# Later layer norms of a two-block transformer kernel: centred rows turned by a product with a diagonal, and the residual made inside the next stage

## The reference

```
first block, layer i in 0..1:
  h = x*(1+sc_m)+sh_m;  y = mixer(h)          # convolutions, 1024-wide products
  x = layer_norm(ALPHA*x + (1+g_m)*y, mix_ln_g[i], mix_ln_b[i])
  h = x*(1+sc_f)+sh_f;  y = mixture_of_32_experts(h)
  x = layer_norm(ALPHA*x + (1+g_f)*y, ffn_ln_g[i], ffn_ln_b[i])
second block, layer l in 0..1:
  x = layer_norm(ALPHA*x + 0.5*swiglu(x, ffn1_in, ffn1_out), ln_g[l,0], ln_b[l,0])
  x = layer_norm(ALPHA*x + hybrid_mixer(x, ...),             ln_g[l,1], ln_b[l,1])
  x = layer_norm(ALPHA*x + 0.5*swiglu(x, ffn2_in, ffn2_out), ln_g[l,2], ln_b[l,2])
layer_norm(v, g, b) = (v - mean(v)) * rsqrt(var(v) + 1e-5) * g + b
```

## Time and profile before

| what | value |
|---|---|
| median of 3 runs | 2887.1 us |
| the profiled execution: its time / its span | 2888.29 us / 2886.5 us |
| TensorE matmul busy | 2541.2 us, 88% |
| VectorE / ScalarE / GpSimd busy | 43% / 29% / 15% |
| mean granted TensorE clock | 0.965 |
| first block / second block in the span | about 0 to 1424 / 1424 to 2886 us |

### The profile page before, as it was taken

One profiled execution on the slowest core, in us unless ns is written; L12 is line 12 of the kernel. 1 busy time (PEld: TensorE's weight loads), 2 busy tenths in 40 slices (PEclk: granted clock), 3 DMA queues, 4 the chain that ended last, 5 costly groups with the idle time before them and its releaser, 6 DMA issues.

```text
span 2886.5 us, 38313 instructions
## 1 busy us (share of the span) xinstructions
PE 2541.2 (88%) x15512; PEld 1772.3 (61%) x15513; DVE 1245.1 (43%) x2035; ACT 844.1 (29%) x1391; POOL 438.0 (15%) x462
## 2 busy tenths in 40 slices
PE   6989888988697888888699899988989989998997
PEld 3653322322584322332299788878979978887897
DVE  5562212110655111210254675556455467555645
ACT  2231100010231100001144344444444434444443
POOL 2210000000210010000020222333012032233301
PEclk9999999999897999999999999999999989999899
DMA  9979999999643999999855453344545535334552
GB/s 350 335 304 393 393 394 394 394 393 394 204 173 130 394 394 394 393 394 393 317 176 187 131 161 118 117 146 162 189 146 184 195 122 166 109 117 142 166 185 73
DMA packets 388354, 716.18 MB, mean 248 GB/s; under 512 B 18881, under 2 KB 192625, under 8 KB 382033
## 3 DMA queue, kind: packets, MB, share of 16 engines
q1 hardware_dynamic: 384048, 707.77, 68.6%
q10 hardware_dynamic: 2336, 3.52, 0.4%
q0 software_dynamic: 1792, 2.42, 0.3%
HBM read 709.69 MB, written 1.05 MB: 246 GB/s over the span
## 4 chain that ended last, share of the span: by engine, by line
PE 51%; DMA 27%; DVE 7%; issue 7%; POOL 5%; ACT 1%; SPq 1%; ACTq 0%; DVEq 0%; POOLq 0%
DMA ring<-in_e_w_down_dram 25%; PE w L702 17%; PE y L714 10%; PE w L706 8%; PE w L913 5%; PE w L899 2%; DMA ring<-in_ada_w_dram 2%; PE w L1150 1%; PE y L940 1%; DVE vv L1373 1%; DVE small L1364 1%; SPq L636 1%; POOL arena L2399 1%; PE w L1135 1%; PE w L882 1%
## 5 line engine op out<-in xcount | busy, mean ns | idle before, releaser
L1262 DVE TENSOR_TENSOR wsp<-ring,wsp 128x1024 fp32r<-128x1024 f32 x464 | 607.0, 1313 | 400.9 <-ACT wsp L1251 400.6
L702 PE MATMUL w<-hh,wsp 128*128 128x256 f32 x5056 | 685.2, 289 | 27.0 <-DVE wsp L1262 18.7
L702 PEld LDWEIGHTS w<-hh,wsp 128*128 128x128 f32 x5056 | 650.5, 196 | 52.5 <-issue 22.6
L1251 ACT CAST wsp<-ring 128x1024 fp32r<-128x1024 f32 x470 | 489.3, 1045 | 401.1 <-PE w L706 249.7
L899 PE MATMUL w<-ring,arena 128*64 128x512 f32 x2048 | 474.2, 600 | 64.9 <-DMA ring<-in_e_w_up_dram 57.4
L706 PE MATMUL w<-hl,wsp 128*128 128x256 f32 x2528 | 358.5, 284 | 5.4 <-DVE hl L1318 5.4
L899 PEld LDWEIGHTS w<-ring,arena 128*64 128x64 f32 x2048 | 135.8, 136 | 368.0 <-issue 213.5
L706 PEld LDWEIGHTS w<-hl,wsp 128*128 128x128 f32 x2528 | 328.4, 193 | 6.8 <-DVE hl L1318 6.8
L913 PE MATMUL w<-ring,ht 128*64 128x512 f32 x1024 | 245.4, 601 | 60.6 <-DMA ring<-in_e_w_down_dram 59.5
L714 PE MATMUL y<-wsp,zsp 128*128 128x512 f32 x1056 | 256.1, 392 | 5.8 <-DVE wsp L1262 3.9
L2124 ACT ACTIVATE ht<-w 128x256 f32<-128x256 f32 x64 | 24.5, 383 | 776.1 <-PE w L899 776.1
(11 more groups left out here) (284 smaller groups left out, 2342.4 us busy)
## 6 DMA issues: line engine op xcount, KB each, us to landing
ring<-in_e_w_gate_dram SPq DMA_DIRECT2D x256, 512.0 KB, 10.2
ring<-in_e_w_up_dram SPq DMA_DIRECT2D x256, 512.0 KB, 11.4
ring<-in_e_w_down_dram SPq DMA_DIRECT2D x128, 1024.0 KB, 13.7
ring<-in_ffn_in_dram SPq DMA_DIRECT2D x88, 1024.0 KB, 5.2
ring<-in_w_in_dram SPq DMA_DIRECT2D x50, 1024.0 KB, 5.2
ring<-in_ada_w_dram SPq DMA_DIRECT2D x48, 1024.0 KB, 11.1
ring<-in_ffn_out_dram SPq DMA_DIRECT2D x44, 1024.0 KB, 4.9
ring<-in_b_w_in_dram SPq DMA_DIRECT2D x12, 1024.0 KB, 12.0
```

What stands on the lines that cost most here:

```text
L702: pe.matmul(dst, a[:, kc * m:(kc + 1) * m], hh[:, kc, :], start=kc == 0 and j == 0, stop=False)
L1251: ac.copy(shaped(halves(i)[0], u.shape), u.cut(ring[:, u.piece % NSLOT, :])).then_inc(*mark("w_high", i))
L1262: e.tensor_tensor(shaped(lo, u.shape), u.cut(ring[:, u.piece % NSLOT, :]), shaped(hi, u.shape).bitcast(F32), ALU.subtract).then_inc(*mark( ...
```

## The change

What it does, for the norms `ffn1` to `n12` (the diff calls them `later`):

- VectorE no longer centres and scales a row in one pass. It centres a half and multiplies it by the gain, which now lies in `lnp` unscaled (`centre`), and makes a 128 x 128 diagonal of the tokens' factors (`diagonal`, in the tile `ht`). TensorE multiplies the centred rows by the diagonal (`to_feature_later`), so the product turns and scales at once.
- ScalarE adds the bias per feature and rounds to `hh` in 16 pieces of 128 x 128, VectorE makes `hl` in 16 pieces (`lows_later`). The passes into `ht` and all of GpSimd's part but the power are gone. The first two projections of a stage run as four runs of products in another order (`first_two`).
- The residual is kept without ALPHA (the norm's epsilon is divided by ALPHA squared for it) and is made by VectorE, four pieces of 128 x 512, inside the next stage: at k = 2 to 5 in `ffn`, at the 2nd to 5th feature projection in `hybrid`. SyncE's wait before the load of `lnp` is now for the last of these.
- For all norms the addition of epsilon goes from GpSimd to VectorE; the last three rows of a stage run bank by bank, (t, h) = (0,0), (0,1), (1,0), (1,1), each with a signal of its own (`y_part`), instead of t by t.
- The last norm's output leaves in four transfers of 128 x 512 instead of two of 128 x 1024.

```
-            def row(key, k, n, i, zh, zl, t, started=False):
+            def last_rows(key, n, i0, z_of):
+                for t in range(2):
+                    for h in range(2):
+                        for k in range(n - 3, n):
+                            i = i0 + k - (n - 3)
+                            if (t, h) == (0, 0):
+                                pe.wait_ge(*low_done(i))
...
+                            ins = row_half(k, n, i, *z_of(k), t, h)
+            def to_feature_later(n):
+                for t in range(2):
+                    pe.wait_ge(*at("diag", n, t))
+                    for f in range(KC):
+                        if f % 4 == 0:
+                            pe.wait_ge(*at("centred", n, t, f // 4))
+                        ins = pe.matmul(turned_at(n, t, f), vv[:, t, f * P:(f + 1) * P], dg[:, t, :], start=True, stop=True)
...
+            def first_two(dsts, i, n):
...
+                            pe.wait_ge(*at("h_hi", n, 1, kc))
...
+                            pe.wait_ge(*at("h_lo", n, kc, 1))
...
-                half(0, 0)
-                half(0, 1)
-                stats(0)
-                scale(0)
-                half(1, 0)
-                half(1, 1)
-                stats(1)
-                weight_lows(ve, "v", prime)
-                scale(1)
+                for t in range(2):
+                    half(t, 0)
+                    half(t, 1)
+                    stats(t)
+                    guard(t)
+                    if n in later:
+                        centre(t, 0)
+                        if n != last_norm:
+                            diagonal(t)
+                        centre(t, 1)
...
+            def lows_later(n):
+                for f in range(KC):
+                    for t in range(2):
+                        ve.wait_ge(*at("h_hi", n, t, bank_end(t, f)))
+                        ve.scalar_tensor_tensor(hl[:, f, t * P:(t + 1) * P], turned_at(n, t, f), h_bias[n][:, f:f + 1],
...
+                    if 2 <= k < 6:
+                        new_x(n, *divmod(k - 2, 2))
...
-                weight_lows(po, "g", prime)
```

More of the change, by code:

```diff
@@ L47 @@
 SHM, SCM, GM, SHF, SCF, GF = range(6)
-Unit = namedtuple("Unit", "piece cut shape low")
+Unit = namedtuple("Unit", "piece cut shape")
 def split_const(value, parts, bits):
@@ L426, in want_hybrid @@
                         "vc": (2816, 128, 0)}
-            n = 0
             for step in projs:
-                low = "g" if n == 1 else "v"
-                n += 1
                 if step[0] == "feat":
@@ L566, in program @@
         last_norm = norms[-1]
+        later = norms[norms.index("ffn1"):]
+        h_bias = {"ffn1": colr("ffn_ln_b", 8, 8)}
+        for l in range(DEPTH):
+            for j in range(3):
+                h_bias[f"n{l}{j}"] = colr("ln_b_2", 8 * (3 * l + j), 8)
         def ada_sum(l, cb):
@@ L581, in low_done, with x_done, turned_at, bank_end @@
         def low_done(i):
-            return at("w_low_v" if units[i].low == "v" else "w_low_g", i)
+            return at("w_low", i)
+        def x_done(n):
+            return at("x_made", n, 1, 1) if n in later else at("x_new", n, 1)
+        def turned_at(n, t, f):
+            if t == 0:
+                return YB[f // 4][:, f % 4 * P:f % 4 * P + P]
+            spare = WB[2:4] if n in ("n00", "n10") else WB[1:3]
+            return [YB[2], YB[3], *spare][f // 2][:, f % 2 * P:f % 2 * P + P]
+        def bank_end(t, f):
+            return f | (1 if t else 3)
         def hi_done(n, u):
@@ L623, in sync_engine @@
                     if before >= 0:
-                        sp.wait_ge(*at("x_new", norms[before], 1))
+                        sp.wait_ge(*x_done(norms[before]))
                     else:
@@ new lines, in row_half, with row @@
+                for j, (a, z) in enumerate(((wh, zh), (wl, zh), (wh, zl))):
+                    ins = pe.matmul(YB[2 * t + h][:, :], z[:, t * P:(t + 1) * P], a[:, h * 512:(h + 1) * 512],
+                                    start=k == 0 and j == 0, stop=k == n - 1 and j == 2)
+                return ins
+            def row(k, n, i, zh, zl):
+                for t in range(2):
+                    for h in range(2):
+                        ins = row_half(k, n, i, zh, zl, t, h)
+                ins.then_inc(*mark("w_used", i))
@@ L739, in mixer_a, with out_rows @@
+            def out_rows(key):
+                i0 = first[key]
+                for k in range(KC - 3):
+                    pe.wait_ge(*low_done(i0 + k))
+                    pe.wait_ge(*at("z_hi", key, k))
+                    pe.wait_ge(*at("z_lo", key, k))
+                    row(k, KC, i0 + k, hh[:, k, :], hl[:, k, :])
+                last_rows(key, KC, i0 + KC - 3, lambda k: (hh[:, k, :], hl[:, k, :]))
             def mixer_a():
@@ L1072, in free_proj @@
                     return WB[p % 2]
+                assert [s[0] for s in projs[0:2]] == ["feat", "feat"]
                 for s in steps:
-                    if s[0] in ("feat", "dup"):
+                    if s == projs[0]:
+                        first_two([free_proj()[:, 0:T] for u in range(2)], i, n)
+                        i += 2
+                    elif s == projs[1]:
+                        pass
+                    elif s[0] in ("feat", "dup"):
                         b = free_proj()
-                        proj(b[:, 0:T], i, n, s == steps[0])
+                        proj(b[:, 0:T], i, n, False)
                         i += 1
@@ L1226, in tensor_engine @@
             moe(1, "mix1")
-            to_feature("ffn1", vv)
+            to_feature_later("ffn1")
             before = "ffn1"
@@ L1329, in to_feature, with norm @@
                 low(3)
-            def norm(n, gate, prime):
+            def norm(n, gate):
                 key = y_of[n]
                 nx = norms.index(n) - 1
+                plain = gate is not None
                 def half(t, h):
@@ L1368, in stats, with guard @@
                     ve.bn_aggr(mv[:, t, :], st[:, t, :, :].rearrange("p a b -> p (a b)")).then_inc(*mark("norm_v", n, "mean", t))
+                def guard(t):
+                    ve.wait_ge(*at("norm_v", n, "mean", t))
+                    ve.tensor_scalar(ve_[:, t:t + 1], mv[:, t, 1:2], EPS / ALPHA ** 2 if plain else EPS, None, ALU.add).then_inc(
+                        *mark("guarded", n, t))
                 def scale(t):
@@ L1748, in hybrid @@
                         i += 1
+                        if s[0] == "feat" and 2 <= i - first[key] and made_x < 4:
+                            new_x(n, *divmod(made_x, 2))
+                            made_x += 1
                     elif s[0] == "gate":
@@ L1913, in vector_engine @@
             mixer_a()
-            norm("mix0", None, 0)
+            norm("mix0", None)
             fold_mix = [colr("mix_ln_g", 8 * l, 8) for l in range(2)], [colr("mix_ln_b", 8 * l, 8) for l in range(2)]
-            fold_ffn = [colr("ffn_ln_g", 8 * l, 8) for l in range(2)], [colr("ffn_ln_b", 8 * l, 8) for l in range(2)]
             fold("mix0", fold_mix[0][0], fold_mix[1][0], 0, SCF, SHF)
@@ L1924, in vector_engine @@
             spread(1, 0, (0, 1))
-            norm("mix1", None, 0)
+            norm("mix1", None)
             fold("mix1", fold_mix[0][1], fold_mix[1][1], 1, SCF, SHF)
@@ L2461, in start @@
         def start(name):
-            made.update({"s": 0, "v": 0, "g": 0} if sig.now is None else {})
+            made.update({"s": 0, "v": 0} if sig.now is None else {})
             sig.now = name
```

303 lines of the change are left out of this document (153 added, 150 removed).

## The result

The changed kernel takes 2841.3 us (median of 4 runs, 2839.32 to 2842.3), the kernel before 2885.4 beside it (4 runs, 2883.33 to 2888.89): a ratio of 0.9845, with a 95% interval of 0.9828 to 0.9862. Executed again on another chip it took 2841.8 (5 runs, ratio 0.9837, 0.9824 to 0.9851). The forecast was 2839, in a range of 2825 to 2858, so it came out right. The profiled execution took 2841.55 us with a span of 2839.8, 46.7 less than the span before.

The account below looks back on a forecast made before the run. It took the stretch from the rows' end to the second projection's end, 20.8 us at n00 for about 6.2 of products, as the bound. 45.4 + 3.9 - 1.6 = 47.7 us saved gave a median of 2839, range 2825 to 2858.

Parts of the forecast that it names:

- The sum of the norms: Six norms, ffn1 to n11: 9.9 at ffn1, 7.5 at n00 and 7.0 at each other, 45.4 us saved.
- Its price is nothing extra: Turning at the norms: a plain float32 product with the diagonal costs 0.11 us, no more than a transpose's 0.12.
- this rival: Turning: a plain product costs four transposes, eight take 3.8 us, giving back 8 us over six norms; no chance given.
- Rows bank by bank: Stage ends: 6 products instead of 12 precede the wait, so at n00 TensorE's rows end 1.43 us later.
- the rival in which it stays up: TensorE's gap before the second turning: the clock does not fall, 8 us more saved, 2831 us; chance 0.20.
- The small pieces: First two projections: ScalarE's 16 pieces come every 0.30 us, VectorE's 16 of `hl` every 0.21, hidden behind the low products.
- The rival of dear pieces: At the norms: ScalarE's pieces cost 0.40, VectorE's 0.35, so 9 to 18 us are lost, 2853 us; chance 0.19.
- ffn1: 9.9: At ffn1 the second projection ends 8.8 us earlier and 1.1 comes back behind it: 9.9 us saved.
- The last norm: 3.9: At the last norm the output is issued at 2878.3 instead of 2882.14, 3.9 us earlier.
- The early norms: Epsilon on VectorE saves 0.2 per norm, bank-by-bank rows lose 1 at mix0 and mix1: -1.6 us, bounds -3 to +1.
- SyncE's load of lnp: Swiglu stages: the load waits for the residual's last piece at k=5, yet stays hidden by 2 to 3 us.
- The ring rival: Swiglu stages: the ring's 12th piece lands late behind lnp, TensorE waits 18 us in each of four, 2911 us; chance 0.03.

Follow-up runs that it names:

- run 4: The changed kernel with the last three rows of a stage run tile by tile again, signals per bank kept: 2833.6 us, ratio 0.9815.
- run 1: The changed kernel with the product by the diagonal replaced by a transpose, without the tokens' factors: 2839.0 us, ratio 0.9835.
- run 9: The changed kernel with the residual's four pieces one step later in each swiglu stage (k = 3 to 6): 2877.9 us, ratio 0.997.

## Why the prediction was right, point by point

- **The sum of the norms held, 45.0 for 45.4, but through errors that cancel, which is in part luck.** (42.6 from join to join, and the 2.4 us by which n12's own join is later, which the prediction put into the last norm.) The mechanism is as told: from the old end of the rows to the second projection's end I gave 15.1 us; the trace has 15.6 at n00, 14.2 at n02, 16.6 at n10.
- **"Its price is nothing extra" is the step that failed.** The prediction read the 16 instructions of the earlier trace rows as 16 products. They are 8: `spread` makes 8 products a call, and L680 has 64 instructions in the trace of its four calls. A product is 0.23 to 0.25 us, not 0.11. The Trainium skill, TensorE: Matmul & The Clock Gate, section Terms, has transpose mode four times faster for FP32; the traces have twice the instructions, and 2.06 against 1.10 us for eight, so it pointed the right way with too large a factor. The cost was 2.5 us of the 8 that this rival gave, since ScalarE's pieces set the pace anyway.
- **Rows bank by bank.** "A wait of 2.4" is 2.31, and the join of t=1 is 0.41 us later than in the old order where the clock stays up, as in my walk (0.3). Not foreseen: the longer wait lets the clock fall *in the rows*. This made 4.4 us of the lost 7.4, and run 4, in which it does not happen, is 8.2 us shorter. That the last bank "is not waited for" was right, but half of it: the order also fills bank (0,1) later, 0.67 us per norm.
- **The clock in the gap.** I had it fall before each second turning and stay down until 6.6 us behind its start, and gave 0.20 to the rival in which it stays up. It stayed up at n00 and n02. At n01, n10 and n11 it fell only when the turning had run for 1.2 to 1.4 us, and for 3.4 us, where the kernel before has 10.2 at n00. So the difference is 0.95 us per norm, not 1.7: the truth lay between, 8 us was too much. The Trainium skill, same page, Part 4: PE-mode transpose, would have transposes count less for the gate than products. No run here tells that apart: with transposes (run 1) the clock fell 0.5 to 1.6 us behind the start of the turning at all five norms from n00 to n11, but the gap is longer too, 3.5 us; with products it fell there at one to five of these five, run by run.
- **The small pieces.** ScalarE's are 0.376 long and 0.26 to 0.27 apart (I took 0.30), VectorE's 0.34 and 0.26 (I took 0.21, bounds to 0.35). `hl` is the limit where the clock stays up, as the rival had it: the last 16 products take 2.33 us instead of 2.08. This is one of the signs that I had named for being wrong: at n00 the last piece of `hl` ends at 1645.84, the low products at 1645.06. The rival of dear pieces (2853) is out.
- **The power.** 0.57 became 0.99, since centring now runs beside it, and VectorE idles 0.44 us behind. I had only reckoned that GpSimd "now has nothing else". Nor is every pass of VectorE free of GpSimd: at n00 the first piece of the residual takes 1.23 us beside the rotations' passes on GpSimd, the second 0.74.
- **ffn1: 9.9 was over-sized through a wrong row.** The one at 1454.07 in the earlier trace rows belongs to the third projection; the second ended at 1452.08. The measured gain is 5.9 from the join, 0.4 lost before it and 1.7 behind it: 7.2.
- **The last norm: 3.9 was under-sized.** From its join on, 7.0 are won. Before, GpSimd's passes stretched VectorE's to 2.82 and 3.17 us; the new four end 3.05 us after the join:

```profile
2833.79 0.21 DVE L1424 BATCH_NORM_AGGREGATE small<-small 128x2 f32<-128x12 f32 x1
...
2835.43 1.41 DVE L1469 SCALAR_TENSOR_TENSOR xa<-vv,small,lnp 128x512 f32<-128x512 f32 x2
```

  and the kernel ends 2.9 us behind them, where it ended 4.4 behind the output's issue at 2882.14. I had counted the smaller last transfer as nothing. Less the 2.4 of its later join, 4.6.
- **The early norms**, -1.6: not settled. The 2.9 lost before the first join is inside the scatter of that block.
- **SyncE's load of lnp.** "Hidden, by 2 to 3 us" is hidden by 0.9 in the first swiglu stage. The ring rival did not come, and TensorE does not wait at k=7; but run 9 shows its mechanism and its weight: once in each of four stages, and the clock on top.

So the largest share that the runs show is that GpSimd's passes are gone from beside VectorE's: 7 to 9 us by moving one pass in the old kernel, 13 lost by giving the residual back, together about half of the 44. The order of the first two projections is worth 6 or 7, the diagonal 1.6 to 3, and the order of the rows costs 8. How the rest, some 20 us, divides among the dropped passes into `ht`, the shorter list on VectorE ahead of the second turning, the finer signals and the last norm's smaller transfers was not tried.

## What to carry to other kernels

An idle engine is not a free one: before work is put on GpSimd "because it has nothing to do", look in the trace for the duration of VectorE's passes alone and beside it. A wait of TensorE has a second price, the products behind it at half clock, so that 1.4 us more wait can cost as much again; try such orders on the chip. And when a row prices a new operation, count its instructions against the number of calls in the code.

## What the runs showed of the hardware that I had not expected

- A plain 128 x 128 product of float32 by float32 is two instructions, a transpose one; eight take 2.06 and 1.10 us to the end of the last.
- GpSimd's power on 128 x 1 takes 0.57 us alone and 0.99 beside a VectorE pass over two SBUF tensors; its 128 x 256 subtraction 0.74 and 1.39. A diagonal of 128 x 128 on VectorE takes 0.29 alone and 0.72 beside GpSimd.
- At the ends of swiglu stages, the clock fell in the rows behind a wait of 2.31 us in 15 of 28 cases, behind 2.02 us in 2 of 4, and behind 0.66 to 1.00 us in none of 16. After 7.59 us of idle time it was at 0.50 from the first product on, and twelve took 5.29 us instead of 2.91:

```profile
1509.50:1511.00 1.50, 1.47 (x4) 1.18 (x5) 0.00 (x0) 0.82 (x1) 0.00 (x0) 0.50 1.09 348
1511.00:1513.00 2.00, 2.00 (x6) 1.61 (x5) 1.56 (x2) 0.60 (x3) 0.00 (x0) 0.50 1.08 394
```
